# Returning the experts' outputs to token order with the places stationary, and finishing the norm on rows

## The reference, cut to what matters

```
u      = modulate(rmsnorm(x, norm_ffn_g), shift, scale)      # T x D
group  = argmax of 4 group logits of u; each token goes to one group
w[8]   = weights of the 2 best of the 8 experts of that group
moe    = sum over the chosen experts of w_e * swiglu_e(u)     # experts: D -> 256 -> D
x      = x + gate * moe                                       # gate: one value per feature
out    = x * rsqrt(mean(x*x over D) + eps) * final_norm_g
```

## Time and profile before

| | |
|---|---|
| median of 3 runs | 2506.0 us (2505.88 to 2506.99) |
| profiled execution | 2505.72 us, its span 2504.3 us, 1.4 us around it |
| TensorE matmul | busy 2413.2 us, 96% of the span |
| VectorE, ScalarE, GpSimd busy | 1409.3, 1193.5, 294.3 us |
| routing after the last projection | from 2183.4 to 2207.6 us of the span |
| experts | 2207.6 to 2481.7 us |
| end | 2481.7 to 2504.3 us |

### The profile page before, as it was taken

The page is one execution under the profiler, slowest core; times in us unless marked ns, Lnnn a source line. Parts: engine busy times, 40 slices in busy tenths (PEclk is TensorE's granted clock), DMA queues, the critical chain, the costliest instruction groups (busy, mean ns, idle before and its releaser), DMA issues.

```text
span 2504.3 us, 52401 instructions
## 1 busy us (share of the span) xinstructions
PE 2413.2 (96%) x23215; PEld 2085.4 (83%) x23215; DVE 1409.3 (56%) x2208; ACT 1193.5 (48%) x1725; POOL 294.3 (12%) x417
## 2 busy tenths in 40 slices
PE   7999999999999999999999999999999888999998
PEld 7999888799999998878899995687477777778787
DVE  5655544376646655533566557453534554378886
ACT  5434465544444434475454436431244442277775
POOL 0100000031101100000211000372123322000000
PEclk9999999999999999999999999999999999999999
DMA  8764522366656654413367522201111011479995
GB/s 256 244 211 152 203 83 92 116 202 202 227 194 202 216 203 160 167 70 119 127 204 255 194 97 101 69 4 40 68 36 37 24 50 41 134 250 365 368 362 183
DMA packets 269445, 396.15 MB, mean 158 GB/s; under 512 B 9624, under 2 KB 173133, under 8 KB 269085
## 3 DMA queue, kind: packets, MB, share of 16 engines
q1 hardware_dynamic: 267481, 389.32, 45.6%
q0 software_dynamic: 1120, 2.17, 0.3%
q10 hardware_dynamic: 612, 1.24, 0.1%
HBM read 391.66 MB, written 1.05 MB: 157 GB/s over the span
## 4 chain that ended last, share of the span: by engine, by line
PE 83%; DVE 6%; DMA 5%; ACT 3%; issue 2%; POOL 0%; SPq 0%; ACTq 0%; DVEq 0%; POOLq 0%
PE ps L282 82%; DMA RB<-in_moe_w_up 5%; DVE gwl L447 2%; ACT gwh L438 1%; DVE wl L447 0%; PE ps L1146 0%; ACT wh L438 0%; DVE AR L657 0%; ACT AR L2898 0%; DVE AT L1231 0%; DVE AR L1967 0%; PE ps L541 0%; ACT AR L2890 0%; ACT AT L1200 0%; DMA VR<-in_diff_gain 0%
## 5 line engine op out<-in xcount | busy, mean ns | idle before, releaser
L447 DVE TENSOR_TENSOR wl<-RB,wh 128x2048 fp32r<-128x2048 f32 (+5 forms) x189 | 412.5, 2186 | 284.8 <-ACT wh L438 284.3
L282 PE MATMUL ps<-H,RB 128*128 128x256 f32 (+2 forms) x1728 | 452.8, 421 | 2.8 <-ACT AR L2869 1.3
L438 ACT ACTIVATE wh<-RB 128x2048 fp32r<-128x2048 f32 (+5 forms) x189 | 342.2, 1815 | 232.6 <-PE ps L282 203.1
L282 PEld LDWEIGHTS ps<-H,RB 128*128 128x128 f32 (+1 forms) x1728 | 320.2, 189 | 114.9 <-issue 77.0
L282 PE MATMUL ps<-xhf,wl 128*128 128x256 f32 x1408 | 403.0, 286 | 3.7 <-DVE xlf L686 3.7
L282 PE MATMUL ps<-xlf,wh 128*128 128x256 f32 x1408 | 399.5, 284 | 0.0
L282 PE MATMUL ps<-xhf,wh 128*128 128x256 f32 x1408 | 399.4, 284 | 0.0
L282 PE MATMUL ps<-AR 64*64 64x64 f32 (+3 forms) x8296 | 258.3, 231 | 40.9 <-issue 24.0
L282 PEld LDWEIGHTS ps<-AR 64*64 64x64 f32 (+2 forms) x8296 | 225.1, 138 | 79.3 <-issue 64.3
L282 PEld LDWEIGHTS ps<-xhf,wl 128*128 128x128 f32 x1408 | 271.3, 193 | 14.2 <-issue 10.1
L282 PEld LDWEIGHTS ps<-xlf,wh 128*128 128x128 f32 x1408 | 271.4, 193 | 0.1
(11 more groups left out here) (445 smaller groups left out, 4105.3 us busy)
## 6 DMA issues: line engine op xcount, KB each, us to landing
RB<-in_ffn_w_gu SPq DMA_DIRECT2D x88, 1024.0 KB, 7.8
RB<-in_w_in SPq DMA_DIRECT2D x23, 2048.0 KB, 7.7
RB<-in_ffn_w_down SPq DMA_DIRECT2D x16, 2048.0 KB, 7.8
RB<-in_w_gate SPq DMA_DIRECT2D x16, 2048.0 KB, 8.7
RB<-in_moe_w_gate SPq DMA_DIRECT2D x32, 1024.0 KB, 7.6
RB<-in_moe_w_up SPq DMA_DIRECT2D x32, 1024.0 KB, 10.2
RB<-in_moe_w_down SPq DMA_DIRECT2D x32, 1024.0 KB, 8.0
RB<-in_ada_w SPq DMA_DIRECT2D x12, 2048.0 KB, 9.9
```

The source lines that it names most:

```text
L282: return M.matmul(o, lhsT, rhs, start=start, stop=stop, skip_group_check=True)
L438: S.activation(self.pair(h)[0], of(slot_of(*key)), ACT.Copy).then_inc(*did("high", *mark))
L447: V.tensor_tensor(lo, of(slot_of(*key)), hi.bitcast(F32), ALU.subtract).then_inc(*did("low", *mark))
```

## The change

1. **End on rows.** The back product has `BACK` (the places) stationary, 128 tokens at a time, and the kept expert output moving, 512 columns: for each of 2 token halves and 2 feature halves, 4 groups by 2 parts, 32 matmuls instead of 64. Groups 0 to 2 of all four banks come first, group 3 last. The result has tokens on the partitions. The transposes and the sum of squares by matmul are gone.
2. **x by rows.** VectorE copies the four banks of transposed x to `XR` during `places_dve`, behind the low parts of k = 3, 5, 6 and 7.
3. **Gate by rows.** Two products `gate_row` of four matmuls each (a column of `MOD` broadcast as the stationary, identity moving, 128 columns) give the gate on all partitions; one stands ahead of the wait for `grouped`, the other ahead of that for `chosen`. ScalarE copies both out, ahead of the exponential of the group logits.
4. **keep** now multiplies by the gate first: VectorE takes each bank times `GATE` to `GY`; ScalarE's copy to the high part waits for that, and VectorE's subtraction for ScalarE's copy.
5. **Norm on rows.** VectorE adds x, ScalarE squares with a running sum, one root, one reciprocal; GpSimd multiplies half the tokens with the gain row and VectorE the other half; ScalarE and VectorE scale. The gain row comes by a GpSimd DMA broadcast to 128 partitions (0.5 MB), issued once the routing's logits exist.

```diff
@@ Route
+                self.XR = H[:, 0, :].rearrange("p (t n) -> p t n", t=2)
+                self.GATE, self.GAIN = H[:, 1, 0:1024], H[:, 1, 1024:2048]
+            def gate_pe(self, o):
+                ps = bank(("gate_row", o), ("gate_rows", o), among=(0, 1, 2))
+                for c in range(4):
+                    ins = mm(ps[:, 128 * c:128 * c + 128], MOD[:, 40 + 4 * o + c, 0:1].broadcast_to([128, 128]), ident,
+                             True, True)
+                ins.then_inc(*did("gate_row", o))
             def places_pe(self):
+                self.gate_pe(0)
...
                 PE.wait_ge(*at("grouped"))
...
+                self.gate_pe(1)
                 PE.wait_ge(*at("chosen"))
@@ places_act, behind the four copies to UT
+                for o in range(2):
+                    AC.wait_ge(*at("gate_row", o))
+                    S.activation(self.GATE[:, 512 * o:512 * o + 512], ps_of("gate_row", o), ACT.Copy).then_inc(
+                        *did("gate_rows", o))
@@ places_dve
                     low_x(k)
                     if k == 4:
                         self.ws_g.low(3)
+                    else:
+                        t, c = {3: (0, 0), 5: (1, 0), 6: (0, 4), 7: (1, 4)}[k]
+                        DV.wait_ge(*at("turned", "u", t, c))
+                        V.tensor_copy(self.XR[:, t, 128 * c:128 * c + 512], ps_of("turned", "u", t, c)).then_inc(
+                            *did("x_rows", t, c))
+            def places_pool(self):
+                PO.wait_ge(*at("route"))
+                P.dma_start(self.GAIN, A["final_norm_g_2"].partition_broadcast(128)).then_inc(*did("gain_rows", by=16))
@@ gathered, scalar(), keep
-                        AC.wait_ge(*at("ed", 8 * e + 7))
                         for o in range(2):
-                            S.activation(xh[:, 4 * o:4 * o + 4, 128 * e:128 * e + 128], ps_of("y", e, o).rearrange(
+                            AC.wait_ge(*at("y_gated", e, o))
+                            S.activation(xh[:, 4 * o:4 * o + 4, 128 * e:128 * e + 128], GY[:, o].rearrange(
                                 "p (c n) -> p c n", c=4), ACT.Copy).then_inc(*did("yk_high", e, o))
@@ gathered, vector(), keep
+                        DV.wait_ge(*at("ed", 8 * g + 7))
...
+                            V.tensor_tensor(GY[:, o], ps_of("y", g, o), route.GATE[:, 512 * o:512 * o + 512],
+                                            ALU.mult).then_inc(*did("y_gated", g, o))
                         for o in range(2):
                             DV.wait_ge(*at("yk_high", g, o))
-                            V.tensor_tensor(xl[own], ps_of("y", g, o).rearrange("p (c n) -> p c n", c=4),
+                            V.tensor_tensor(xl[own], GY[:, o].rearrange("p (c n) -> p c n", c=4), xh[own].bitcast(F32),
@@ class RowFinish
+            def pe(self, xh, xl):
+                where = [(t, o) for t in LAT for o in range(2)]
...
+                for groups in ((0, 1, 2), (3,)):
+                    for t, o in where:
+                        ps = ps_of("at_home", t, o).rearrange("p (c n) -> p c n", c=4)
+                        for g in groups:
+                            PE.wait_ge(*at("y_kept", g, o))
+                            for part in (xl, xh):
+                                ins = mm(ps, self.back[:, g, 128 * t:128 * t + 128],
+                                         part[:, 4 * o:4 * o + 4, 128 * g:128 * g + 128], g == 0 and part is xl,
+                                         g == 3 and part is xh)
...
+            def act(self):
+                S.activation(self.ms, EPS, ACT.Sqrt).then_inc(*did("root", "end_g", 0))
+                for t in LAT:
+                    for o in range(2):
+                        AC.wait_ge(*at("row_x", t, o))
+                        S.activation(self.SQ[:, 2 * t + o], self.YO[:, t, 512 * o:512 * o + 512], ACT.Square,
+                                     accum_out=self.ss[:, t, o:o + 1]).then_inc(*did("row_squared", t, o))
+                AC.wait_ge(*at("row_sum"))
...
+                S.activation(self.ms, self.ms, ACT.Sqrt, bias=EPS[:, 0:1], scale=1.0 / DM).then_inc(*did("root", "end_g"))
+                AC.wait_ge(*at("rstd", "end_g"))
+                for o in range(2):
+                    AC.wait_ge(*at("row_gain_p", o))
...
+            def pool(self):
...
+                    PO.wait_ge(*at("row_squared", 0, o))
+                    own, cols = self.YO[:, 0, 512 * o:512 * o + 512], slice(512 * o, 512 * o + 512)
+                    P.tensor_tensor(own, own, self.route.GAIN[:, cols], ALU.mult).then_inc(*did("row_gain_p", o))
+            def dve(self):
+                for t in LAT:
+                    for o in range(2):
+                        DV.wait_ge(*at("at_home", t, o))
+                        cols = slice(512 * o, 512 * o + 512)
+                        V.tensor_tensor(self.YO[:, t, cols], ps_of("at_home", t, o), self.route.XR[:, t, cols],
+                                        ALU.add).then_inc(*did("row_x", t, o))
...
+                DV.wait_ge(*at("row_squared", 1, 0))
...
+                V.tensor_tensor(own, own, self.route.GAIN[:, 0:512], ALU.mult).then_inc(*did("row_gain", 0))
+                DV.wait_ge(*at("row_squared", 1, 1))
...
+                V.tensor_tensor(self.ms, self.ss[:, :, 0], self.ss[:, :, 1], ALU.add).then_inc(*did("row_sum"))
...
+                V.tensor_tensor(own, own, self.route.GAIN[:, 512:1024], ALU.mult).then_inc(*did("row_gain", 1))
+                DV.wait_ge(*at("root", "end_g"))
+                V.reciprocal(self.rs, self.ms).then_inc(*did("rstd", "end_g"))
```

More of the change, by code:

```diff
@@ L3282, in pe @@
                     if c % 4 == 0:
-                        bank(("turned", "u", t, c), ("u_rows", t, c), among=(4, 5, 6, 7))
+                        bank(("turned", "u", t, c), ("u_rows", t, c), ("x_rows", t, c), among=(4, 5, 6, 7))
                     ps = ps_of("turned", "u", t, c // 4 * 4)
@@ L3463, in experts @@
             route.places_dve()
+            route.places_pool()
             area, rank, cmb = route.area, route.rank, route.cmb
@@ L3489, in gathered @@
             S1, CW, BACK = area(4096, 4, T), area(5120, 4, 8), sb("gbk", STAGE, [4, T], F32R)
-            end = Finish(area, "g")
+            GY = sb("gy", o + 22528, [2, 512])
+            end = RowFinish(area, route, BACK)
             order = expert_order()
@@ L3528, in tensor @@
                         if n == 0:
-                            outs[g] = [bank(("y", g, o), ("y_kept", g, o), among=kept) for o in range(2)]
+                            outs[g] = [bank(("y", g, o), ("y_gated", g, o), among=kept) for o in range(2)]
                         hi, lo = ws.weights(downs[e])
@@ L3540, in tensor @@
                 PE.wait_ge(*at("back", 2))
[L3542 to L3552, removed]
+                end.pe(xh, xl)
             def scalar():
@@ L3600, in vector @@
                         g = e
+                        DV.wait_ge(*at("ed", 8 * g + 7))
+                        DV.wait_ge(*at("gate_rows", 1))
+                        for o in range(2):
+                            if g:
+                                DV.wait_ge(*at("y_kept", g - 1, o))
+                            V.tensor_tensor(GY[:, o], ps_of("y", g, o), route.GATE[:, 512 * o:512 * o + 512],
+                                            ALU.mult).then_inc(*did("y_gated", g, o))
                         for o in range(2):
@@ L3603, in vector @@
                             DV.wait_ge(*at("yk_high", g, o))
-                            V.tensor_tensor(xl[own], ps_of("y", g, o).rearrange("p (c n) -> p c n", c=4),
-                                            xh[own].bitcast(F32), ALU.subtract).then_inc(*did("y_kept", g, o))
-                for c in range(KD):
-                    DV.wait_ge(*at("spread", c))
-                    V.scalar_tensor_tensor(out=XT[:, c, :], in0=ps_of("spread", c)[:, 0:T], scalar=MOD[:, 40 + c, 0:1],
-                                           in1=XT[:, c, :], op0=ALU.mult, op1=ALU.add).then_inc(*did("moe_in", c))
+                            V.tensor_tensor(xl[own], GY[:, o].rearrange("p (c n) -> p c n", c=4), xh[own].bitcast(F32),
+                                            ALU.subtract).then_inc(*did("y_kept", g, o))
                 end.dve()
@@ L3614, in gathered @@
             vector()
+            end.pool()
             end.store()
@@ L3736, in vector @@
                 end.dve()
-            everyone(("xm_low", 7), ("low", "g", 2), ("xm", 7), ("expert_exp",), ("combined",))
+            everyone(("xm_low", 7), ("low", "g", 2), ("xm", 7), ("expert_exp",), ("combined",), ("x_rows", 1, 4), ("gain_rows",))
             tensor()
```

34 lines of the change are left out of this document (added).

## The result

The changed kernel takes 2513.27 us (median of 20 runs) beside 2508.78 us for the kernel before in the same sittings (20 runs): a ratio of 1.0022, 95% interval 1.0016 to 1.0028, so 4.0 to 7.0 us slower. The forecast was 1.1 us faster, and its range ended 1.7 us above before. The profiled execution took 2513.45 us, span 2511.7, mean granted clock 0.991 (before: 2505.72, 2504.3, 0.993).

A forecast was written before the change was run, and what follows sets the result against it. Bound by DMA, with TensorE also full, until keep 2, then TensorE alone. Terms: -4.7 (end) + 2.6 (keep 2) + 1.0 (keeps 0 and 1) + 0 (routing) = -1.1 us, median 2504.9 us; range 2500.8 to 2507.7.

The forecast's parts named there:

- The end: From last expert product to first store: 16.4 us shrinks to 11.3, less 0.4 for contact; gain 4.7 us, bounds 4.2 to 5.6.
- The contact between VectorE and GpSimd: In the end, VectorE's first gain product runs beside GpSimd's second and delays the sum of squares; 0.4 us.
- The stores are the same four: At the kernel's end, the four stores keep their order; no gain or loss was priced for them.
- Keep 2: Last early keep: ScalarE waits for VectorE's gating with two high parts queued behind; TensorE 2.6 us late, bounds 1.2 to 3.4.
- Keeps 0 and 1: Earlier keeps in the experts' stage: delayed loads mostly covered by the queue; 0.5 us each, 1.0 in all, bounds 0 to 5.2.
- An issue that comes up to 2.2 us late costs nothing: Experts' stage until keep 2: each load waits some 2.2 us behind its forerunner, so DMA queueing covers that delay; cost 0.
- rival 3: Every keep pays in full, as late issues empty the DMA queue: 3 x 2.6 - 4.7 = +3.1, 2509.1 us; chance 0.13.
- Rival 2: Experts' stage: the keeps are free, absorbed by the ring and the halves in hand; 2501.3 us; chance 0.10.
- Rival 1: Routing: gate-row matmuls hold the clock at 2.4 GHz, moving everything behind up 2.4 us; 2502.5 us; chance 0.22.
- The routing at 0: In the routing, gate rows, x rows and the gain row's DMA are hidden in waits; cost 0.
- signs announced: First store about 11.7 us after last product; keep 2's low part 2.6 us later; landings 8 to 9; routing clock 0.5 or 1.0.
- three signs that were to show the forecast wrong: TensorE's gap behind a keep under 1 us, gaps between keeps, or the first store later than 13 us.

The follow-up runs named there:

- e3_b_work: Kernel before the change, plus two VectorE products at keeps 0, 1 and 2 that nobody reads and ScalarE doesn't wait for; 4.0 us slower than before (1.0016).
- e4_a_fill: Changed kernel plus 11 unused TensorE matmuls of 512 columns ahead of the down weights after each of keeps 0, 1 and 2; ratio to before 0.9993.
- f3_rows_only: Kernel before the change plus only the routing's additions (gate rows, x by rows, gain DMA), rows unread; 0.8 us faster than before (0.9997).
- f4_now_0: Changed kernel with ScalarE's copies and VectorE's subtractions of keeps 1 and 2 moved behind the next up weight's high part, keep 0 unmoved; 0.9994 of before.
- g2_a_nopool: Changed kernel with the end's gain products moved from GpSimd to VectorE, keeps as in the change; 2.8 us slower than before (1.0011).

## Why the prediction was wrong

**The end: right.** Forecast gain 4.7 us to the first store, measured 4.5 (16.85 to 12.36). The steps came in the order given. The contact between VectorE and GpSimd was there, but elsewhere and dearer: the first gain product took its plain 0.69 us, and the sum behind it 1.22 instead of 0.2, 1.0 us where I had taken 0.4. ScalarE's squares gave 0.4 back: they start 0.62 us apart, not 0.73, since the read-out of a sum overlaps the next pass (the first ends at 2501.85, the pass behind it starts at 2501.75). The Trainium skill (SBUF — State Buffer, "SBUF: two separate sides") has the shared port pair as an exclusive lock, held for the whole instruction. The sum that ends 0.02 us from GpSimd's product, and takes 0.15 us when GpSimd is idle, agrees with that, and not with the 0.4 that I preferred from one pair of rows; so does the other direction, GpSimd's product that began behind VectorE's and took 1.71 us instead of 1.26. "The stores are the same four" missed 0.9 us: from the first store to the end it took 5.26 instead of 6.13. Why was not tested.

**Keep 2: right in kind and size.** The forecast had gating, copies, high part, low part in this order and TensorE 2.6 us late; the gap went from 0.41 to 2.75. It used the right reason too: ScalarE's queue. The two tests of that reason, over keeps 0 to 2 together, gave +8.8 us (the wait alone) and -4.3 (the copies moved). It isn't the only way: VectorE's added work without ScalarE's wait makes gaps of 1.8 us (e3_b_work).

**Keeps 0 and 1: a step that failed.** "An issue that comes up to 2.2 us late costs nothing", and so 0.5 us were taken per keep. Their gaps are 3.02 and 3.05 us, where they were 0.34 and 0.46: as large as keep 2's. The forecast had it that these keeps reach TensorE by way of late loads, which a queue would cover. They reach it first by the way of keep 2: the weights had landed 3.8 us before ScalarE began on them, so nothing in the queue of loads could cover that wait. The late issue came on top, and there the queue did give something: behind keep 0 the down loads were issued 2.8 us late (2305.58 against 2300.48, less the 2.27 of the later start) and took 6.0 us to landing instead of 8.0. The next gate and up loads were again issued 2.9 us late (2310.83 against 2305.66, less the 2.27), and the up load saved 0.7 (9.2 instead of 9.9). TensorE had only 1.95 us idle in the whole stage to make a delay good with. In all the waiting came to 5.7 us for three keeps (e4_a_fill), against the 3.6 forecast and the 7.8 of rival 3. By which path the 1.9 us came back was not tested.

**The clock: the larger step that failed, a term left at nothing.** I priced TensorE's gap at its length. Behind two of the three gaps the granted clock fell to 0.50, which cost 4.8 us more; the waiting was 2.1 us over its forecast. With both the sum closes: -5.4 for the end, +5.7 for the waiting and +4.8 for the clock make +5.1, where the runs have +4.0 to +7.0. The earlier trace rows had shown the like, a stretch of little work and then the low level; I used them for the routing, where the change adds work, and not for the keeps, where it adds a gap. With the gaps filled the same kernel comes out 1.8 us faster than before (interval -4.3 to +1.0), beside the forecast's -1.1. That these lie so close is luck: the waiting is still larger than forecast there, and by the traces that kernel's stage and end add up to +0.3.

**The rest.** Rival 3 (every keep pays in full, +3.1) stood at 0.13. Its 3 x 2.6 us are the gaps as measured (7.6), though not for its reason, since no load makes them; with the 4.8 us of the clock it comes to +7.9, above the measured +4.0 to +7.0. Rival 2 fell. Rival 1 (the clock holds in the routing) fell: 0.50 from 2190 on, in spite of 16 products of 128 columns. The page named there (the Trainium skill, TensorE: Matmul & The Clock Gate, "What's actually happening") says that the clock follows recent activity; that agrees with e4_a_fill, and it bore on the keeps more than on the place where I cited it. The routing at 0 was right (f3_rows_only). Of the signs announced, the gap at keep 2 came, and landings of 9.2 us behind keep 0 and 8.2 behind keep 1; the first store was forecast 11.7 us behind the last product and came 11.97 behind that product's end (2494.47). Of the three signs that were to show the forecast wrong none came: none of them looked at how large the gaps of keeps 0 and 1 are, or at the clock behind them.

## What to carry over

Before a copy that runs ahead is made to wait for another engine, read what stands behind it in its own queue: here moving the same work behind two weight parts turned +5.5 us into -4.3. Before a queue of loads is let cover a delay, see on which side of the landing the delay arises: here the weights had been in place for 3.8 us. And price a gap of 2 to 3 us on TensorE in a full stage at its length plus what the clock may take behind it (here 1.5 to 2.8 us where it fell).

## What the runs showed of the hardware that was not expected

- The granted clock can fall to 0.50 behind a single gap in a stage where TensorE is otherwise busy all the time, but not behind every such gap. Six kernels here have 14 gaps of 1.7 to 3.1 us at their keeps, and it fell behind 10 of them. Behind keep 0 it fell in f4_now_0 (gap 3.06) and g2_a_nopool (3.06) and not in the changed kernel (3.02); in e3_b_work (gaps 1.72 to 1.85) it fell behind keep 2 alone, whose 48 products took 12.75 us. In the stage of the seven kernels whose gaps are all 0.70 us or less it never fell. Where it falls, the gap costs 1.5 to 2.8 us more than its length. What decides it was not found out.
- Products whose result nobody reads, put into the gaps (2.78 us of them each), keep the clock at 1.00: the 48 products behind keeps 1 and 2 take 4.4 us less together.
- A sum of two columns on VectorE took 1.22 us beside GpSimd's product, 0.15 without it. GpSimd's product that began during one of VectorE's on SBUF took 1.71 us, the one before it 1.26. VectorE's operations that read PSUM weren't delayed (0.68 beside GpSimd and without).
